# One half of each pair's scatter moved behind the second up product, in a mixture-of-experts stage

## The reference, cut to what matters

```python
def hier_moe(h, w_group, b_group, w_expert, b_expert, w1, w3, w2):
    ...                                   # each token picks 2 of 32 experts, with weights
    def expert_block(args):
        xb, e = args
        return (jax.nn.silu(xb @ w1[e]) * (xb @ w3[e])) @ w2[e]
    yb = lax.map(expert_block, (buf.reshape(n_blk, BLK, d), blk_e))
    y = yb.reshape(n_rows, d)[dest] * sw[:, None].astype(h.dtype)
    return jnp.zeros_like(h).at[stok].add(y)
```

## Time and profile before

| what | value |
|---|---|
| time, median of 3 runs (lowest, highest) | 2791.73 us (2786.26, 2792.19) |
| the profiled execution's own time | 2781.74 us |
| its span in the profile | 2779.6 us |
| PE busy | 2526.8 us (91%) |
| DVE busy | 889.2 us (32%) |
| ACT busy | 403.2 us (15%) |
| moved by the DMA engines, all queues | 587.86 MB, mean 211 GB/s |
| loads of the expert weights, `ring<-in_w` | 384 of 1024 KB, 8.4 us from issue to landing (median) |

### The profile page before, as it was taken

How to read it: one execution, slowest core, us unless ns; L and a number is a source line. 1 busy time by engine, 2 the same in 40 slices (tenths; PEclk the granted TensorE clock), 3 DMA queues, 4 the chain that set the end, 5 groups by cost and what they waited for, 6 DMA issues and landing times.

```text
span 2779.6 us, 30325 instructions
## 1 busy us (share of the span) xinstructions
PE 2526.8 (91%) x11446; PEld 1423.9 (51%) x11446; DVE 889.2 (32%) x1782; ACT 403.2 (15%) x964; POOL 85.6 (3%) x106
## 2 busy tenths in 40 slices
PE   5989979999999997998799999998789999879998
PEld 3458464444454444446543433444567844466853
DVE  2666233232232335626322222223361101371000
ACT  1025120000000001013200100001241000141000
POOL 1200000000000001200000000000000000000000
PEclk8999979999999998999899999999899999999999
DMA  7520208988889884210199999993403443402441
GB/s 273 182 91 1 91 31 333 362 343 345 347 353 370 354 332 152 91 61 1 61 386 393 415 381 409 413 392 138 152 2 124 155 159 117 143 29 91 151 166 69
DMA packets 143285, 587.86 MB, mean 211 GB/s; under 512 B 9185, under 2 KB 19425, under 8 KB 93921
## 3 DMA queue, kind: packets, MB, share of 16 engines
q1 hardware_dynamic: 142768, 584.55, 54.7%
q10 hardware_dynamic: 288, 1.19, 0.1%
q0 software_dynamic: 144, 0.97, 0.1%
HBM read 585.63 MB, written 1.05 MB: 211 GB/s over the span
## 4 chain that ended last, share of the span: by engine, by line
PE 76%; DMA 9%; DVE 8%; issue 3%; ACT 2%; POOL 1%; SPq 1%; DVEq 0%; ACTq 0%; POOLq 0%
PE psum L1858 13%; PE psum L1625 10%; DMA ring<-in_w 8%; PE psum L2054 8%; PE psum L2067 8%; PE psum L1844 7%; PE psum L1871 6%; PE psum L1921 5%; PE psum L1558 4%; PE psum L1972 3%; PE psum L1693 3%; PE psum L1718 3%; PE psum L1617 2%; PE psum L1564 1%; POOL rstd L375 1%
## 5 line engine op out<-in xcount | busy, mean ns | idle before, releaser
L1858 PE MATMUL psum<-ring,arena 128*64 128x512 f32 x2048 | 465.5, 602 | 38.4 <-DMA ring<-in_w 36.2
L1625 PE MATMUL psum<-ring,hT 128*128 128x512 f32 x832 | 362.5, 593 | 5.0 <-issue 1.6
L1858 PEld LDWEIGHTS psum<-ring,arena 128*64 128x64 f32 x2048 | 150.2, 138 | 346.2 <-issue 316.5
L1625 PEld LDWEIGHTS psum<-ring,hT 128*128 128x128 f32 x832 | 155.9, 190 | 195.0 <-issue 190.6
L1255 DVE TENSOR_TENSOR arena<-arena,psum 128x512 f32<-128x512 f32 x204 | 140.2, 687 | 331.5 <-PE psum L1871 331.5
L1921 PE MATMUL psum<-ring,arena 128*64 128x512 f32 x1024 | 226.8, 595 | 0.0
L2067 PE MATMUL psum<-ring,arena 128*128 128x512 f32 x512 | 220.3, 592 | 3.2 <-DVE arena L1456 3.2
L2054 PE MATMUL psum<-hT,ring 128*128 128x256 f32 x1024 | 221.5, 379 | 1.3 <-DVE hT L1321 1.3
L2054 PEld LDWEIGHTS psum<-hT,ring 128*128 128x128 f32 x1024 | 194.4, 190 | 28.0 <-DVE hT L1321 1.7
L1844 PE MATMUL psum<-arena 128*128 128x128 f32 x1632 | 200.6, 281 | 8.7 <-DVE arena L1243 8.7
L1844 PEld LDWEIGHTS psum<-arena 128*128 128x128 f32 x1632 | 191.7, 196 | 28.4 <-issue 28.4
(11 more groups left out here) (246 smaller groups left out, 1875.3 us busy)
## 6 DMA issues: line engine op xcount, KB each, us to landing
ring<-in_w SPq DMA_DIRECT2D x384, 1024.0 KB, 8.4
ring<-in_w_ff SPq DMA_DIRECT2D x64, 1024.0 KB, 5.2
ring<-in_w_mod SPq DMA_DIRECT2D x32, 1024.0 KB, 7.7
hT<-in_w_mod SPq DMA_DIRECT2D x16, 1024.0 KB, 10.1
ring<-in_w_in_c SPq DMA_DIRECT2D x12, 1024.0 KB, 5.7
ring<-in_w_in SPq DMA_DIRECT2D x12, 1024.0 KB, 5.4
ring<-in_w_out SPq DMA_DIRECT2D x8, 1024.0 KB, 5.1
ring<-in_w_in_ab SPq DMA_DIRECT2D x6, 1024.0 KB, 5.0
```

The lines of the kernel that those rows point to most:

```text
L1625: inst = pe.matmul(bank, hT[:, k, P * m:P * m + P], w[k], start=k == 0, stop=k == KB - 1)
L1858: inst = pe.matmul(out[64 * e:64 * e + 64, :], xgT[:, b, k, 64 * e:64 * e + 64], m, start=k == 0, stop=k == KB - 1)
```

## The change

`add_pair` takes the tiles it is to do. Of the pair's nt tiles the first half is done where the whole was, between the two up products, and the second half behind the second up product: behind `folded` and ahead of the gather on PE, and behind the product with the SiLU (and behind `with_bias`) on DVE. The two waits at the head of PE's `add_pair` stay with the first half alone. The last scatter, behind the loop, is still done in one piece. No instruction of work is added or removed, and the banks are used in the same order by both engines.

```diff
@@ DVE
-                def add_pair():
-                    for tile in range(nt):
+                def add_pair(parts):
+                    for tile in parts:
                         for h in range(2):
                             dve.wait_ge(mm_v, jobs.next())
@@
                     for b in range(2):
-                        add_pair()
+                        add_pair(range(nt // 2))
                         if l == 0 and b == 1:
                             dve.wait_ge(mod_product, mod_in.next())
@@
                             with_bias(1, i, psum[:, 7, :]).then_inc(mod_taken, 1)
                             dve.wait_ge(mod_taken, so_far(mod_taken))
+                        add_pair(range(nt // 2, nt))
                         dve.wait_ge(mm_v, jobs.next())
@@
-                add_pair()
+                add_pair(range(nt))
@@ PE
-                def add_pair():
-                    pe.wait_ge(v_free, v_done.value())
-                    pe.wait_ge(a_free, a_done.value())
-                    for m in range(nt):
+                def add_pair(parts):
+                    if 0 in parts:
+                        pe.wait_ge(v_free, v_done.value())
+                        pe.wait_ge(a_free, a_done.value())
+                    for m in parts:
                         for h in range(2):
                             pe.wait_ge(v_free, v_done.value(back=3))
@@
                         up(psum[:, 4, :], b)
-                        add_pair()
+                        add_pair(range(nt // 2))
                         if l == 0 and b == 1:
                             pe.wait_ge(mod_loaded, mod_in.next(2))
@@
                             folded(psum[:, 7, :], mod_sums).then_inc(mod_product, 1)
                             mod_out.n += 1
+                        add_pair(range(nt // 2, nt))
                         pe.wait_ge(pick_ready, picks.next())
                         gather(1 - b, 0)
@@
-                add_pair()
+                add_pair(range(nt))
```

## The result

The changed kernel takes **2819.49 us** in the median (2814.13 to 2828.11), the kernel before 2791.96 us. The ratio is 1.0103, with a 95% interval of 1.0071 to 1.0135. The profiled execution took 2817.48 us with a span of 2815.3 us, 35.7 us more than the span before. So the kernel became about 1% slower.

A forecast was written before the change was run, and what follows sets the result against it. PE, busy but waiting on late ring loads, was taken as the bound. Layer 0's 21.8 us plus layer 1's 6 us made 28 us (1.0%), added to the 2791.7 us median: 2820 us, range 2804 to 2831.

The forecast's parts named there:

- What bounds the kernel, and which view decides: Both expert loops: PE busy, waiting 36.2 us for ring loads; one pair's timeline beside its loads' landing times decides.
- The slack of 0.8 us in hand for c7 in layer 0, b = 1: Second up product before the change: c7 lands at 778.9 us and is needed at 779.7, so no wait.
- Layer 0, forecast 21.8 us: Eight pairs with b = 1 wait for c5 and c7: seven lose 2.6 us, the first 3.44 us.
- the whole 3.44 us: Layer 0's first b = 1 pair: c7 already makes PE wait, so the moved half scatter's full 3.44 us is lost.
- Layer 1, forecast +6 us with half absorbed: 15 pairs wait 0.8 us each for c7, 12 us; the nearly always busy load queue gives half back.
- this second part: Layer 1: smaller waits at k = 4 might avoid PE's clock falls; with all absorbed, bound of 5 us gained.
- What stays the same, forecast 0: Both loops: still three changes of weight width per pair, VectorE's evictions covered, other loads issued as before; cost 0.
- The bound given with it: One exposed weight-load start more or less in each of 32 pairs: at most 0.8 x 32 = 26 us.
- Rival 1: Scatter's VectorE eviction really holds the second up product; half a burst gains up to 18.2 us, 2774 us; chance 6%.
- Rival 2: PE's clock falls at layer 0's new b = 1 waits, 14 us on top, 2834 us; chance 8%.
- Rival 3: DMA queue alone sets the loop in both layers, new waits replace old: 2790 to 2794 us; chance 5%.
- Rival 4: Layer 1 absorbs nothing, 2826 us, or all, 2809 to 2814 us; within the forecast's width, no separate chance.

The follow-up runs named there:

- the three split loops: Layer 0 loops of the changed kernel, its second profile, and the kernel before with the scatter split in layer 0 alone: 648.9, 649.0 and 649.2 us.
- the three whole ones: Layer 0 loops of the kernel before, its second profile, and the kernel before with the scatter split in layer 1 alone: 619.2, 625.6 and 624.9 us.
- the other kernels: Scatter split in layer 0's b = 0 pairs alone (2785.34 us); mod loads behind c1 in the changed kernel (2791.47 us) and in the kernel before (2792.66 us).
- the five whole loops: Layer 1 loops in profiles of kernels whose layer 1 scatter is in one piece, as in the kernel before: 499.5, 497.5, 493.0, 497.1 and 493.1 us.
- the four split ones: Layer 1 loops in profiles of kernels whose layer 1 scatter is split as in the changed kernel: 502.1, 502.3, 502.7 and 500.9 us.
- The later set of runs: The changed kernel run again, unaltered, beside the kernel before on the same chip: 2814.17 us, ratio 1.0082.
- the two halves alone: The kernel before with the scatter split in layer 0 alone (2809.8 us, ratio 1.0065) or in layer 1 alone (2794.51 us, ratio 1.0019).

## Why the prediction was right

**What bounds the kernel, and which view decides: right.** The step that carried the result was to set each chunk's landing against the moment at which PE would need it. The slack of 0.8 us in hand for c7 in layer 0, b = 1, was used up, with the waits that were forecast:

| place | forecast, us each | after, us each | sum after |
|---|---|---|---|
| layer 0, b = 1, c5 | 1.2 | 1.28 (8 times) | 10.3 |
| layer 0, b = 1, c7 | 1.4 | 1.31 (8 times) | 10.5 |
| layer 0, b = 0 | 0 | 0 | 0 |
| layer 1, c7 | 0.8 | 0.80 (15 times) | 11.9 |

The forecast gave each wait as landing minus need, and the rows give it from the modelled end of the last matmul, which is later. Like for like the waits were 0.05 to 0.14 us longer than forecast. In the pair above c5 was 792.00 - 788.84 - 1.85 = 1.31 us late and c7 796.96 - 792.00 - 3.51 = 1.45 us. In the pair of layer 1 c7 was 1653.38 - 1648.93 - 3.51 = 0.94 us late.

**Layer 0, forecast 21.8 us: right in kind, a little too small.** The stretch that the forecast worked out, from the half product at k = 4 to the gather, grew by 2.9 us in each of the seven pairs with b = 1 behind the first, where 2.6 us were forecast. The terms that make it up are read from the pair above: 1.31 and 1.45 us of lateness, 0.07 us because a half product behind a wait takes 3.58 us (800.54 - 796.96) and not 3.51, and 0.08 us because the two half scatters take 3.63 + 3.52 us and the whole one 7.07. The first pair, for which the forecast had the whole 3.44 us, also grew by 2.9 us only (from 20.91 to 23.80): its wait at k = 4 was 1.74 instead of 0.92 us, and so c7 landed 15.8 instead of 16.4 us behind the half product. Together that is 23.3 us. In the pairs with b = 0 the stretch grew by 0.1 us, and from the gather to the next pair it shrank by as much.

This fits the 23.8 us between the loops that were not lucky. That the very first pair of profiles gave 29.6 us is the early landing of c3 in the profile of before. The forecast said that this execution was 10 us under the median but not why; 6 us of it were at k = 4 in layer 0. Over all, the three split loops waited 18.4 us there on the mean and the three whole ones 15.4 us; the other kernels had 16.2, 16.7 and 19.2 us there, so no effect of the change shows.

**Layer 1, forecast +6 us with half absorbed: the number right, by two misses that cancelled.** The forecast had 12 us of cost and 6 us given back. A pair became 1.01 us longer and not 0.8, which is 15.2 us for 15 pairs, so 9.3 us must have come back to leave 5.9 us. The profiles show two parts. The waits at k = 4 were 24.5, 24.3, 21.1, 23.7 and 21.6 us in the five whole loops and 17.0, 17.2, 17.0 and 15.9 us in the four split ones, 6.3 us less on the mean. And nine half products ran slow, at 5.1 to 5.35 us, in the five whole loops (two of the first profile's three are in the earlier trace rows), against one in the four split ones; at 1.7 us each that is 2.6 us for a loop. The forecast had this second part only as a bound. The two make 8.9 us, so the sum closes to 0.4 us. The close hit in this layer is luck; the mechanism is not.

The reason given for the absorption, that the later issue of c2' and c3' finds less in front of it, can be read from the traces. When c2' is issued, c1' still needs 2.2 to 2.4 us to land in the whole loops and 1.3 us in the split ones (means over 15 pairs). c3' lands 7.56 to 7.77 us behind its issue in the whole loops and 7.19 to 7.27 us in the split ones, and 0.43 us of difference in 15 pairs are 6.4 us. The ninth of its 16 steps comes 6.5 to 6.6 us behind the issue in both, so what comes sooner is the last parts of the load.

**What stays the same, forecast 0: right.** The split in layer 0's b = 0 pairs alone is the test (ratio 0.9989). The bound given with it was far too wide: the two changes of tiling around a burst cost PE 3.63 - 3.44 = 0.2 us together by the prediction's own rows, not 0.8 us each. Ahead of the second up product in the earlier trace rows its matmuls start at 1679.66 and 1680.18 us, 0.52 us apart instead of 0.43, while the weight load idles for 0.76 us. VectorE's evictions were hidden: in the pair of layer 1 above the transposes (L1559) follow the gather without a wait.

**The rivals.** Rival 1, the eviction as what holds the second up product, fell by the trace: 18.2 us, 24 times, before and after, with bursts of eight and four or of four and two matmuls. In the changed kernel's layer 1 the row reads as before (weight load, start, us). Behind it stand a change from scatter to gather, which keeps the tiling, and the up product that follows the scatter in the kernel with the scatter at k = 4, where PE awaits no eviction:

```profile
1679.45 0.19 PEld L1873 LDWEIGHTS psum<-arena 128*128 128x128 f32 x1 [0.24 <-issue]
1680.40 0.20 PEld L1859 LDWEIGHTS psum<-ring,arena 128*64 128x64 f32 x4 [0.76 <-DVE arena L1255]
...
804.54 0.19 PEld L1845 LDWEIGHTS psum<-arena 128*128 128x128 f32 x1 [0.24 <-issue]
...
1663.93 0.20 PEld L1860 LDWEIGHTS psum<-ring,arena 128*64 128x64 f32 x4 [0.76 <-issue]
```

The same 0.76 us stand there with no releaser, and without a change of tiling only the usual 0.24 us. So the idle time belongs to the change of tiling, and the name of the releaser was of no meaning. The rule of the Trainium skill's page "TensorEngine Tiling (Array Packing)", section "Key Properties", is that changing the mode drains the engine; the trace agrees with it by these 0.76 against 0.24 us. Rival 2, a clock fall at the new waits, did not happen in either layer (granted clock 1.00 in both windows, its level of 2.4 GHz). The rule named there, of the Trainium skill's page "TensorE: Matmul & The Clock Gate", Part 1, that the throttled state is the default and activity releases it, is not tested by these loops, in which the clock stayed up. Rival 3, no change, fell with the result. Rival 4, layer 1 with nothing or all absorbed, was within the range, and the 5.9 us lay between.

**The sum against the median.** 28 us were forecast and 27.5 us is the difference of the medians (2819.49 - 2791.96). The later set of runs gives 0.82% or 23 us by the ratio and 27 us by the medians, and the two halves alone 18 and 5 us by the ratio. The loops of the profiles give 23.8 and 5.9 us, 30 us together. So the close hit owes something to chance, and the effect is better told as 23 to 30 us.

## What to carry to other kernels

For work that is moved past a matmul that reads streamed weights, write down for each chunk when it lands and when the engine will then need it: moving work from ahead of the use to behind it eats that slack, and once it is gone the whole rest is paid in a wait, although no instruction was added. The same table tells where work does good: here the scatter at the spot where PE already waited for its chunks made the kernel 0.8% faster. In a loop that hangs on its loads, look also at what the longer lap gives back. Before a trace's releaser is believed, look whether the same idle time stands at a like change of work that has no releaser.

## What the runs showed of the hardware that was not expected

- A wait that a trace shows inside a stream of matmuls is shorter than what it costs. An up product takes 7.02 us in one piece and 7.24 us beside a wait of 1.30 us in its middle. Of the 0.22 us 0.15 lie ahead of the wait, since the row counts it from the modelled end of the last matmul (3.66 against 3.51 us), and 0.07 behind it (3.58 us).
- The waits at k = 4 in an unchanged loop differ by 6 us between executions (11.3 and 17.7 us in layer 0), with the issues at the same points. The ninth of a load's 16 steps comes at 6.5 to 6.6 us for c3 in both layers of all kernels whose scatter is not at k = 4; the last comes at 6.9 to 7.8 us, and the wait follows it. Why the last parts come when they do was not found.
- TensorE's clock fell to its lower level behind waits of 2.26, 2.26 and 3.16 us in layer 1 of the first profile of before, two of them in the earlier trace rows (granted clock 0.69 from 1641.00 to 1646.50 us, and 1.00 in the 4 us ahead), and not behind those of 2.24 and 2.18 us in the same loop. In the four split loops one half product ran slow, behind 2.29 us; all other waits there were under 1.8 us.
